# A hybrid attention and mixture-of-experts step: the samples' attention taken batch by batch, with one ring of five key/value buffers and two expert units loaded behind slots 3 and 8

## The chip, the cores and the metric

The kernel runs on one core of a Trainium2 chip. The metric is the device time of one execution in microseconds; the median of three runs of the kernel before is 1143.01 us. TensorE, VectorE, ScalarE and GpSimd compute; SyncE here only issues DMAs, and waits for semaphores before it does.

## The reference, cut to what matters

One layer of a decoder in float32 for 256 prompt tokens and 32 sample tokens (8 batches of 4), with D = 1024.

```python
proj = x_all @ w_in                       # q, k, v of two head groups (A and B), 8 heads of 64 each
oa_p, ob_p = attention(prompt)            # 256 x 256, causal, ALiBi; group B weights dilated patterns
oa_s = attention(q_s, [cache_k[pages], k_s], [cache_v[pages], v_s])       # per batch: 256 past keys + 4 new
ob_s = attention(q_s, [state_k_win, k_s], [state_v_win, v_s])
hx = layer_norm(ALPHA * x_all + head_rmsnorm([oa, ob]) @ w_out)
comb = top4(softmax(hx @ w_router + b_router))
f = sum(comb[:, e] * (swiglu(hx @ w_gate_up[e] + b_gate_up[e]) @ w_down[e] + b_down[e]) for e in range(32))
y = layer_norm(ALPHA * hx + f)
```

The 32 experts' weights are 403 MB and are read once. The 16 key and 16 value blocks of the samples (8 batches, two groups) are 256 x 512 floats each, 512 KB.

## The kernel before, in words

**Attention in slots.** The first stage is written out by hand in 29 slots (`STEPS`, L276). Every engine walks the same slots in order, each with its own part of each. In slots 0 to 23 TensorE makes one eighth-width piece of the projection (`project`, L747, products at L764 and L767, and at L773 for the samples' values in slots 11 and 23); in slots 24 to 28 it multiplies with `w_out` (L925, samples L930). Behind that product, tables (L277 to L284) say what else a slot has: `SCORE`, `TURN`, `MIX`, `MSQ` for the prompt's eight head pairs, `KROWS` for turning key rows that are to be stored (`turn_rows`, L814), and `KEY`, `SAMP_SCORE`, `SAMP_TURN`, `SAMP_MIX` for the samples.

**The samples' attention** comes in four quads: group A or B, and batches 0 to 3 or 4 to 7. A key block `m` (0 to 15) is turned by eight transposes (`turn_keys`, L827, transposes at L737): four of its first 128 positions into PSUM bank 5, four of its other 128 into bank 6. ScalarE copies bank 5 and VectorE bank 6 into `kT[m % 6]` (`copy_keys`, L1469 and L1739). When four blocks are turned, `samp_scores` (L838) makes the quad's scores in one go, 16 matmuls of 256 columns and 16 of 32, each on one of four 32-column tiles of the array, one tile per batch. VectorE adds and takes the maximum, ScalarE exponentiates, VectorE scales (`samp_scale`), TensorE turns the probabilities (`samp_turn`, L860) and ScalarE copies them to `sampPT` (L1489). `samp_mix` (L866) multiplies with the values, 12 matmuls of 512 columns for all eight heads of a batch at once, and VectorE keeps the right head of each row (`samp_take`, L1760): a masked copy over 512 columns and a sum.

**Buffers.** SyncE loads key blocks into a ring of four (`kring`) and values a quad at a time, 2 MB (`vring`, loads 0, 1, 2 to one place and load 3 to the key ring's). These lie over the expert ring: nine slots of 16 KB per partition (`ring`), of which slot 0 holds the values in this stage, slot 1 four of the six `kT`, slots 2 to 4 `xT`, `qkT` and `vtok`, slot 5 the key ring, slots 6 and 7 the weights `wblk` and `wout`.

**The hand-over to the experts.** A unit is 2 MB of expert weights; a pair of experts has 12 units (8 of `w_gate_up`, 4 of `w_down`), and there are 16 pairs. After attention's own loads SyncE issues the first pair's units as their places come free, each behind a wait, in this order: unit 1 when all sample scores are made, 0 when three quads are mixed, half of unit 6 (to a place aside, `first`), 5 when the last quad is mixed, 2 when the last mean squares are made, 3 and 4 when everything that leaves `qkT`, `vtok` and `kstage` has been stored (L557), 9 behind the first residual sums, 7 and 8 when `w_out`'s products are done, the other half of 6, and then 10, 11 and those of the next pair, each when the unit that held its slot has been used (`unit_free`, L569). The product of pair 0 with `w_gate_up` (L1176) begins at 219 us in the profiled execution. From there on all is loops over pairs: gather (L1060), gate and up (L1176), down (L1229), combine (L1256).

**Order around slots 18 to 28.** In slot 19 VectorE takes the reciprocal of the first four pairs' mean squares (`invert_means`, L1788) and scales the first samples' rows (`samp_norm`, L1805). Its key copy stands early in a slot, before the sample sums. In slot 27 two reciprocals over 512 columns (`scale_out`, L1781) follow the last head pair's mixing of slot 26.

Of the kernel before, what the change touches and what calls it, by code (L numbers as in the profile page):

```python
# [16 lines left out]
SEQ = 256  # L17
# [20 lines left out]
KRING, KTURNED = 4, 6  # L38
# [25 lines left out]
def constant_tables():  # L64
# [7 lines left out]
    keep[p, C_HEAD + p // DS % H] = 1  # L72
# [11 lines left out]
    b, h, q = p // NS, p // DS % H, p % DS  # L84
# [25 lines left out]
def build_layer(nc, x_prompt, x_sample, cache_k, cache_v, state_k, state_v, page_table, w_in, gn_moba,  # L110
# [9 lines left out]
    def place(name, shape, at=None, dt=F32):  # L120
# [16 lines left out]
    sampM = place("sampM", [128, G], at=acc_at + 10240)  # L137
# [49 lines left out]
    vring = [place("vring0", [128, 4, 2, G], at=at[0])] * 3 + [place("vring3", [128, 4, 2, G], at=at[5])]  # L187
    kT = [place(f"kT{m}", [128, 4, PAST], at=(at[6] + 24576 if m < 2 else at[1] - 8192) + 4096 * m) for m in range(KTURNED)]
    xT = place("xT", [128, KC, T], at=at[2])
    headPT.append(place("headPT2", [128, 2, 384], at=at[2] + 9216))  # L190
    sampPT = place("sampPT", [128, 2, 3, 128], at=at[2] + 12288)
    square = place("square", [128, SEQ], at=at[2] + 15360)
# [3 lines left out]
    kring = place("kring", [128, KRING, 2, G], at=at[5])  # L196
# [4 lines left out]
    qblk = place("qblk", [128, 2, DB, 4, 32])  # L201
# [4 lines left out]
    sampP = place("sampP", [128, SW])  # L206

# [3 lines left out]
        wout_in2 wout_in3 k_landed0 k_landed1 k_landed2 k_landed3 v_landed0 v_landed1 v_landed2 v_landed3 ln1_in  # L211
# [22 lines left out]
    k_landed = [sems[f"k_landed{i}"] for i in range(KRING)]  # L234
    v_landed = [sems[f"v_landed{i}"] for i in range(4)]
# [40 lines left out]
    SLOTS_P, STEPS = 2 * len(BLOCKS), 29  # L276
    SCORE = {4: 0, 6: 1, 8: 2, 10: 3, 16: 4, 18: 5, 20: 6, 22: 7}  # L277
# [124 lines left out]
    def _(sp):  # L402
# [36 lines left out]
        def load_k(m):  # L439
            if m >= KRING:  # L440
                sp.wait_ge(S.keys_turned, 2 * (m - KRING + 1))
            load_keys(m, (pages_k, win_k), kring[:, m % KRING], k_landed[m % KRING])

        def load_v(q):
            if q in (1, 2):
                sp.wait_ge(S.samp_mixed, q)
            if q == 3:
                sp.wait_ge(S.keys_turned, 32)
            for b4 in range(4):
                load_keys(4 * q + b4, (pages_v, win_v), vring[q][:, b4], v_landed[q])  # L450
# [6 lines left out]
        load_k(0)  # L457
        load_w_in(2)
        for m in range(1, KRING):
            load_k(m)  # L460
        load_v(0)
# [3 lines left out]
        def free_slot(m):  # L465
            return [s for s, n in KEY.items() if n == m - KRING][0]

        for slot in range(1, SLOTS_P):
            for n in range(3, len(BLOCKS)):
                if 2 * (n - 3) + (3 if BLOCKS[n - 3][1:] == (2, 0) else 1) == slot:  # L470
                    load_w_in(n)
            if slot == 19:
                sp.wait_ge(S.projected, 20)
                load_wout(0)
            for m in range(KRING, 16):
                if free_slot(m) == slot:
                    load_k(m)
            if slot in (14, 18):
                load_v(SAMP_MIX[slot] + 1)

# [15 lines left out]
        def load_start(u):  # L496
            load_unit(0, 0, u, slot=start_slot(u))

# [34 lines left out]
        load_v(3)  # L533
# [12 lines left out]
        sp.wait_ge(S.samp_mixed, 4)  # L546
# [110 lines left out]
    def _(pool):  # L657
# [9 lines left out]
        def block_queries(g):  # L667

            pool.wait_ge(S.proj_copied, copied_at(slot_of_tile(g, 0, 3)))
            for j in range(4):  # L670
                for half in range(2):
                    r = slice(64 * half, 64 * half + 64)
                    nc.gpsimd.tensor_copy(
                        qblk[r, g, :, j, 8 * j + 4 * half:8 * j + 4 * half + 4],
                        qkT[r, 8 * g + j, SEQ:T].rearrange("p (b q) -> p b q", b=DB)).then_inc(S.qblk_ready, 1)
# [23 lines left out]
        nc.gpsimd.memset(qblk[:], 0.0).then_inc(S.qblk_ready, 1)  # L699
        pool.wait_ge(S.projected, 4)  # L700
        copy_state(2)
        pool.wait_ge(S.qblk_ready, 1)
# [32 lines left out]
    def _(pe):  # L735
# [78 lines left out]
        def turn_rows(i, slot):  # L814
# [3 lines left out]
            pe.wait_ge(S.keys_copied_act, jobs_to(KEY, slot))  # L818
            if i:
                pe.wait_ge(S.kstage_ready, i)  # L820
            if i == 3:
                pe.wait_ge(S.samp_taken, 3)
# [4 lines left out]
        def turn_keys(m, slot):  # L827
            pe.wait_ge(k_landed[m % KRING], 32 * (m // KRING + 1))
            for c in range(2):
                if m:  # L830
                    pe.wait_ge((S.keys_copied_act, S.keys_copied_dve)[c], m)
                if c == 0 and jobs_to(KROWS, slot):
                    pe.wait_ge(S.kstage_ready, jobs_to(KROWS, slot))
                for j in range(4):
                    ins = turn(bank[5 + c][:, 128 * j:128 * j + 128], kring[:, m % KRING, c, 128 * j:128 * j + 128])
                ins.then_inc(S.keys_turned, 1)

        def samp_scores(q):  # L838

            g, quad = divmod(q, 2)  # L840
            if q == 1:
                pe.wait_ge(S.samp_copied, 2)
            if q == 2:
                pe.wait_ge(S.samp_taken, 2)
            if q == 3:
                pe.wait_ge(S.samp_copied, 6)
            pe.wait_ge(S.qblk_ready, 8 * g + 9)
            pe.wait_ge(S.proj_copied, copied_at(slot_of_tile(g, 1, 3)))
            pe.wait_ge(S.keys_copied_act, 4 * q + 4)
            pe.wait_ge(S.keys_copied_dve, 4 * q + 4)  # L850
            for part in range(2):
                for j in range(4):
                    for b4 in range(4):
                        out = bank[7][32 * b4:32 * b4 + 32, 0:PAST] if part == 0 else bank[7][32 * b4:32 * b4 + 32, PAST:SW]
                        k = kT[(4 * q + b4) % KTURNED][:, j, :] if part == 0 else qkT[:, 8 * g + 4 + j, SEQ:T]
                        ins = nc.tensor.matmul(out, qblk[:, g, 4 * quad + b4, j, :], k, start=(j == 0), stop=(j == 3),
                                               tile_position=(0, 32 * b4))
            ins.then_inc(S.samp_scored, 1)
# [7 lines left out]
        def samp_mix(q):  # L866
            g = q // 2
            pe.wait_ge(S.samp_copied, (4, 4, 6, 8)[q])
            pe.wait_ge(S.vtok_ready, 8 * g + 8)
            pe.wait_ge(v_landed[q], 128)  # L870
            if q == 1:
                pe.wait_ge(S.samp_taken, 1)
            if q == 2:
                pe.wait_ge(S.kstage_ready, 3)
                pe.wait_ge(S.keys_copied_act, 16)
# [17 lines left out]
        def head_mix(n):  # L893
# [6 lines left out]
            elif n:  # L900
                pe.wait_ge(S.keys_copied_dve, 16)
# [1356 lines left out]
```

## Time and profile before

| | us |
|---|---|
| median of three runs | 1143.01 |
| the three runs | 1143.07, 1141.0, 1143.01 |
| span of the profiled execution | 1138.4 |
| TensorE busy | 1100.8 |
| VectorE busy | 293.2 |
| ScalarE busy | 204.1 |
| first product with expert weights starts at | 219.0 |

The profile shows one execution; its span runs from the first to the last instruction, and the runs' times hold some 4.6 us more, at its start and end. Matmuls are pipelined, and a busy TensorE is not TensorE at its peak. TensorE's granted clock is full for nearly the whole span (mean 0.997).

### The profile page before, as it was taken

The page shows a single profiled execution, that of the slowest core. Times are in us where ns is not written, and L with a number is a line of the kernel's source. Part 1 is how long each engine was busy: PE and PEld are TensorE (multiplying, and loading weights), DVE is VectorE, ACT ScalarE, POOL GpSimd, SP SyncE. Part 2 cuts the span into 40 slices and gives each one's busy share as a digit, 9 for nine tenths or more (in the row PEclk, how much of TensorE's full clock was granted, in tenths as well). Part 3 has the DMA queues.
Part 4 walks back from the last instruction along what each step waited for, and adds up shares of the span by engine and source line. Part 5 has one row for each costly group of instructions (what it writes and reads, how often), then busy time and mean ns, then how long its engine had stood idle before and what let it go on. Part 6 is the DMA issues. An engine that isn't in the chain of part 4 may idle for free.

```text
span 1138.4 us, 14132 instructions
## 1 busy us (share of the span) xinstructions
PE 1100.8 (97%) x5468; PEld 462.9 (41%) x5469; DVE 293.2 (26%) x734; ACT 204.1 (18%) x481; POOL 30.2 (3%) x65
## 2 busy tenths in 40 slices
PE   8999999999999999999999999999999999999996
PEld 6876764433333333333333333333333333333331
DVE  1553757530303030212121212121202031303123
ACT  2322412411111120202020202020201111111112
POOL 0110111000000000000000000000000000000001
PEclk9999999999999999999999999999999999999998
DMA  9967778999999999999999999999999999999994
GB/s 361 347 221 247 286 274 344 418 431 408 429 420 425 432 431 430 430 430 431 432 429 431 432 431 432 431 431 431 431 431 432 432 431 431 431 430 430 397 423 192
DMA packets 61348, 454.37 MB, mean 399 GB/s; under 512 B 6595, under 2 KB 19539, under 8 KB 35572
## 3 DMA queue, kind: packets, MB, share of 16 engines
q1 hardware_dynamic: 58818, 440.97, 93.0%
q0 software_dynamic: 1728, 10.75, 2.5%
q10 hardware_dynamic: 754, 1.98, 0.4%
q8 instruction: 34, 0.56, 0.2%
q14 instruction: 14, 0.11, 0.0%
HBM read 450.14 MB, written 11.93 MB: 406 GB/s over the span
## 4 chain that ended last, share of the span: by engine, by line
PE 79%; DMA 16%; ACT 2%; DVE 1%; SPq 1%; issue 1%; DVEq 0%
PE bank L1176 26%; PE bank L1229 19%; DMA ring<-in_w_gate_up 15%; PE bank L737 6%; PE bank L764 6%; PE bank L1060 5%; PE bank L1256 3%; PE bank L1344 2%; PE bank L767 2%; PE bank L925 2%; PE bank L1056 1%; DMA ln_bs<-in_ln_b 1%; PE bank L882 1%; PE bank L1272 1%; ACT ybuf L1448 1%; ACT actT L1448 1%
## 5 line engine op out<-in xcount | busy, mean ns | idle before, releaser
L1176 PE MATMUL bank<-ring,xg 128*64 128x512 f32 x1904 | 417.6, 594 | 11.2 <-DMA ring<-in_w_gate_up 11.2
L1176 PEld LDWEIGHTS bank<-ring,xg 128*64 128x64 f32 x1904 | 137.6, 137 | 282.0 <-issue 279.8
L1229 PE MATMUL bank<-ring,actT 128*64 128x512 f32 x960 | 216.1, 597 | 4.1 <-ACT actT L1448 4.1
L2111 DVE TENSOR_TENSOR acc<-acc,bank 128x512 f32<-128x512 f32 x60 | 41.3, 688 | 484.8 <-PE bank L1256 484.7
L1602 ACT ACTIVATE sig<-gate 128x256 f32<-128x256 f32 x64 | 26.7, 417 | 526.0 <-DVE gate L2093 526.0
L1229 PEld LDWEIGHTS bank<-ring,actT 128*64 128x64 f32 x960 | 67.3, 137 | 119.9 <-issue 115.3
L2093 DVE TENSOR_SCALAR gate<-bank 128x256 f32<-128x256 f32 x64 | 26.9, 420 | 194.8 <-PE bank L1176 175.8
L764 PE MATMUL bank<-xT,wblk 128*128 128x288 f32 x256 | 65.4, 409 | 0.2 <-DVE xT L1701 0.2
L1593 ACT ACTIVATE xg<-bank,small 128x128 f32<-128x128 f32 x128 | 48.1, 457 | 97.0 <-PE bank L737 96.9
L1060 PE MATMUL bank<-hx,pick 128*128 128x512 f32 x128 | 59.2, 605 | 0.0
L1448 ACT ACTIVATE ybuf<-bank 128x512 f32<-128x512 f32 x63 | 36.0, 596 | 126.8 <-PE bank L1229 87.3
L1256 PE MATMUL bank<-ybuf,spread 128*128 128x512 f32 x120 | 58.4, 618 | 0.0
L764 PEld LDWEIGHTS bank<-xT,wblk 128*128 128x128 f32 x256 | 47.4, 190 | 14.6 <-issue 2.7
L1060 PEld LDWEIGHTS bank<-hx,pick 128*128 128x128 f32 x128 | 23.0, 189 | 34.3 <-issue 34.3
L1256 PEld LDWEIGHTS bank<-ybuf,spread 128*128 128x128 f32 x120 | 19.1, 188 | 39.0 <-DVE acc L2111 19.7
L925 PE MATMUL bank<-wout,outT 128*128 128x512 f32 x64 | 29.8, 603 | 0.0
L767 PE MATMUL bank<-wblk,xT 128*128 128x256 f32 x128 | 29.1, 380 | 0.0
L1344 PE MATMUL bank<-ring,xg 128*64 128x512 f32 x128 | 28.3, 595 | 0.0
L2097 DVE SCALAR_TENSOR_TENSOR up<-up,gate 128x256 f32<-128x256 f32 x64 | 27.2, 425 | 3.3
L737 PEld LDWEIGHTS bank<-keep,ybuf 128*128 128x128 f32 x128 | 17.7, 207 | 25.3 <-issue 24.3
L728 POOL TENSOR_TENSOR acc<-acc,ln_b_sb 128x512 f32<-128x512 f32 x2 | 3.0, 1502 | 941.5 <-DVE acc L2217 941.5
L2094 DVE TENSOR_SCALAR up<-bank 128x256 f32<-128x256 f32 x64 | 26.6, 415 | 0.0
(249 smaller groups left out, 707.5 us busy)
## 6 DMA issues: line engine op xcount, KB each, us to landing
ring<-in_w_gate_up SPq DMA_DIRECT2D x119, 2048.0 KB, 26.5
ring<-in_w_down SPq DMA_DIRECT2D x63, 2048.0 KB, 27.3
ring<-in_w_gate_up SPq DMA_DIRECT2D x16, 1024.0 KB, 20.1
wblk<-in_w_in SPq DMA_DIRECT2D x11, 1024.0 KB, 7.8
kring<-in_cache_k_moba SPq DMA_DIRECT2D x16, 256.0 KB, 7.3
vring<-in_cache_v_moba SPq DMA_DIRECT2D x16, 256.0 KB, 7.3
out<-in_state_k_win POOLq DMA_DIRECT2D x8, 512.0 KB, 5.0
out<-in_state_v_win POOLq DMA_DIRECT2D x8, 512.0 KB, 5.9
```

Source lines behind the costliest of these rows:

```text
L737: return nc.tensor.transpose(out, in_, ident[0:in_.shape[0], 0:in_.shape[0]])
L764: ins = nc.tensor.matmul(out[:, 0:T], w[:, k, 128 * c:128 * c + 128], xT[:, k, :], start=(k == 0), stop=(k == KC - 1))
L767: ins = nc.tensor.matmul(out[:, 0:256], xT[:, k, 128 * c:128 * c + 128], w[:, k, :], start=(k == 0), stop=(k == KC - 1))
L925: return nc.tensor.matmul(bank[2 * t + half][:, :], outT[:, k, t0:t0 + rows], wout[:, k, 512 * half:512 * half + 512], start=(k == 0), sto ...
L1060: return nc.tensor.matmul(bank[6 + a][:, :], pick[:, t, :], hx[:, t, 512 * a:512 * a + 512], start=False, stop=(t == 1))
L1176: ins = nc.tensor.matmul(bank[n][64 * e:64 * e + 64, :], xg[:, k, 64 * e:64 * e + 64], w[e][:, 512 * n:512 * n + 512], start=False, stop=( ...
L1229: ins = nc.tensor.matmul(bank[4 + half][64 * e:64 * e + 64, :], actT[:, j, 64 * e:64 * e + 64], w[e][:, at:at + 512], start=(j == 0), stop ...
L1256: ins = nc.tensor.matmul(bank[4 + half][:, :], spread[:, t0:t0 + rows], ybuf[:, 512 * half:512 * half + 512], start=True, stop=True)
L1344: ins = nc.tensor.matmul(bank[n][64 * e:64 * e + 64, :], xg[:, k, 64 * e:64 * e + 64], w[:, at:at + 512], start=False, stop=(k == KC - 1))
L1448: return nc.scalar.activation(out, in_, ACT.Copy, **kw)
L1593: ins = nc.scalar.activation(xg[:, k, :], turned, ACT.Identity, bias=s_(c_cols + KC + k), scale=s_(c_cols + k))
L2111: V.tensor_tensor(o, o, new, ALU.add).then_inc(S.added, 1)
```

## The change

Scores and mixing go batch by batch. The four tiles of the array now hold the four head pairs of one batch, where they held the four batches of a quad. So a key block can be scored as soon as it is turned (`KSCORE`), two `kT` buffers do, and a value block can be used when it lands. Keys and values share one ring of five 512 KB buffers, `kv`; four of them lie where the key ring lay, one in the ninth slot. A buffer is loaded when the use five places earlier in the list `KV_USED` is over. The products with the values are 36 matmuls of 128 columns a quad, in two parts (`MIX_FIRST`, `MIX_LAST`). Both halves of a key block go through bank 5: the first behind the slot's projection, the second at the slot's end, after ScalarE has copied the first. VectorE's key copy moves to the end of the slot. Slots 0 and 1 of the expert ring are free in this stage, and SyncE issues unit 0 in its slot 3 and unit 1 in its slot 8.

```diff
-KRING, KTURNED = 4, 6
+KVRING, KTURNED = 5, 2
...
+    EARLY_UNITS = {3: 0, 8: 1}
-    KEY = {1: 0, 2: 1, 3: 2, 4: 3, 5: 4, 6: 5, 10: 6, 11: 7, 13: 8, 15: 9, 16: 10, 17: 11, 19: 12, 20: 13, 21: 14, 22: 15}
-    KROWS = {8: 0, 12: 1, 14: 2, 25: 3, 26: 4, 27: 5}
-    SAMP_SCORE, SAMP_TURN = {9: 0, 12: 1, 20: 2, 23: 3}, {10: 0, 13: 1, 21: 2, 24: 3}
-    SAMP_MIX = {14: 0, 18: 1, 24: 2, 26: 3}
+    KEY = {4: 0, 5: 1, 7: 2, 8: 3, 9: 4, 10: 5, 12: 6, 14: 7, 15: 8, 16: 9, 18: 10, 19: 11, 20: 12, 21: 13, 22: 14, 23: 15}
+    KSCORE = {7: (0,), 8: (1,), 9: (2,), 10: (3,), 12: (4,), 13: (5,), 14: (6,), 15: (7,), 18: (8,), 19: (9,), 20: (10, 11),
+              22: (12,), 23: (13,), 24: (14, 15)}
+    KROWS = {11: 0, 13: 1, 17: 2, 24: 3, 25: 4, 26: 5}
+    SAMP_SUM, SAMP_TURN = {10: 0, 15: 1, 20: 2, 24: 3}, {11: 0, 16: 1, 21: 2, 25: 3}
+    MIX_FIRST, MIX_LAST = {12: 0, 17: 1, 22: 2, 26: 3}, {13: 0, 18: 1, 23: 2, 26: 3}
+    MIX_AT = ((6, 0), (6, 0), (6, 0), (7, 384))
...
# SyncE
+        def load_kv(n):
+            v, m, _ = KV_USED[n]
+            if n >= KVRING:
+                v_before, before, _ = KV_USED[n - KVRING]
+                if v_before:
+                    sp.wait_ge(S.samp_mixed, before // 2 + 1)
+                else:
+                    sp.wait_ge(S.keys_turned, 2 * before + 2)
+            load_keys(m, ((pages_k, win_k), (pages_v, win_v))[v], kv[n % KVRING], kv_landed[n % KVRING])
...
-        load_v(3)
         sp.wait_ge(S.projected, SLOTS_P)
         load_wout(1)
         load_wout(2)
-        sp.wait_ge(S.samp_scored, 4)
+        sp.wait_ge(S.samp_scored, 16)
         load_wout(3)
-        load_start(1)
-        sp.wait_ge(S.samp_mixed, 3)
-        load_start(0)
...
# TensorE
+        def turn_keys(m, c, slot):
+            if c == 0:
+                pe.wait_ge(*kv_in(0, m))
                 if m:
+                    pe.wait_ge(S.keys_copied_dve, m)
+                if jobs_to(KROWS, slot):
                     pe.wait_ge(S.kstage_ready, jobs_to(KROWS, slot))
+            else:
+                pe.wait_ge(S.keys_copied_act, m + 1)
+            for j in range(4):
+                ins = turn(bank[5][:, 128 * j:128 * j + 128], kv_of(0, m)[:, c, 128 * j:128 * j + 128])
+            ins.then_inc(S.keys_turned, 1)
...
+            for j in range(4):
+                ins = nc.tensor.matmul(bank[7][32 * j:32 * j + 32, 0:PAST], qblk[:, quad, window(b4, j)], kT[m % KTURNED][:, j, :],
+                                       start=(b4 == 0), stop=False, tile_position=(0, 32 * j))
...
+            for b4 in (2 * part, 2 * part + 1):
+                pe.wait_ge(*kv_in(1, 4 * q + b4))
+                for c in range(2):
+                    for j in range(4):
+                        ins = nc.tensor.matmul(out[32 * j:32 * j + 32, :], sampPT[:, c, window(b4, j)],
+                                               kv_of(1, 4 * q + b4)[:, c, 128 * j:128 * j + 128],
+                                               start=(b4 == 0 and c == 0), stop=False, tile_position=(0, 32 * j))
...
# TensorE's order within a slot: project, turn_keys(m, 0), scores, mean squares, head scores, turn_rows,
# samp_turn, mixing parts, head_turn, head_mix, spread_means, turn_samples, turn_keys(m, 1)
+            if slot in KEY:
+                turn_keys(KEY[slot], 1, slot)
...
# ScalarE and VectorE, before the copy of key block m
-                act.wait_ge(S.samp_scored, (m - KTURNED) // 4 + 1)
+                act.wait_ge(S.samp_scored, m - KTURNED + 1)
...
# VectorE, in samp_take
-            link(V.tensor_reduce(otS[:, q, :], sampM[:, :].rearrange("p (h d) -> p d h", h=H), AXX, ALU.add))
+            link(V.tensor_tensor(otS[:, q, :], sampM[:, 0:64], sampM[:, 64:128], ALU.add))
...
# VectorE, last in its slot
+            if slot in KEY:
+                copy_keys(KEY[slot])
```

The lines that begin with # say where a piece stands. The tables that hold batch and head numbers, and GpSimd's copies of the queries into `qblk` (four larger ones for eight), follow the new order of rows.

## Rows read from the trace of the kernel before

**Rows 1.** The page: TensorE's busy time, and GB/s in 40 equal slices.
```profile
PE 1100.8 (97%) x5468; PEld 462.9 (41%) x5469; DVE 293.2 (26%) x734; ACT 204.1 (18%) x481; POOL 30.2 (3%) x65
...
GB/s 361 347 221 247 286 274 344 418 431 408 429 420 425 432 431 430 430 430 431 432 429 431 432 431 432 431 431 431 431 431 432 432 431 431 431 430 430 397 423 192
```
**Rows 2.** TensorE's longest wait up to 215 us and from 660 us: us, times, longest.
```profile
PE bank L737 <- DMA keep<-in_keep_table: 4.9, 1, 4.9
...
PE bank L1176 <- DMA ring<-in_w_gate_up: 11.2, 11, 1.3
```
**Rows 3.** Windows: length, engines' busy us, then TensorE's clock, DMA share, GB/s.
```profile
194.00:196.00 2.00, 2.00 (x5) 0.57 (x3) 1.86 (x7) 0.00 (x0) 0.00 (x0) 1.00 0.00 0
...
660.00:1095.00 435.00, 419.49 (x1868) 150.52 (x1864) 79.45 (x186) 60.08 (x137) 0.00 (x0) 1.00 1.01 428
```
**Rows 4.** SyncE's timeline at the hand-over (start us, us), and one of its waits.
```profile
158.41 7.40 SPq L494 DMA_DIRECT2D ring<-in_w_gate_up  x2
...
183.86 12.42 SPq L494 DMA_DIRECT2D ring<-in_w_gate_up  x3
...
222.61 0.37 SPq L494 DMA_DIRECT2D ring<-in_w_down  x1
...
SPq L557 <- DMA out<-kstage: 11.0, 1, 11.0
```
**Rows 5.** Tile `ring`, time from issue to landing: unit 3 (195.4 us), unit 10 (222.6 us).
```profile
DMA to landing us min/median/max: 7.2/7.2/7.2
...
DMA to landing us min/median/max: 8.0/8.0/8.0
```
**Rows 6.** The chain in order of time in the attention stage: start us, us, what.
```profile
80.13 2.16 PE bank L856 x62
...
93.54 2.84 PE bank L882 x24
...
108.64 3.88 PE bank L764 x16
...
114.85 4.08 PE bank L764 x16
...
153.29 1.88 PE bank L773 x64
```
**Rows 7.** Tiles `kT` (ScalarE) and `sampM` (VectorE): duration ns min/median/max.
```profile
L1448 ACT ACTIVATE kT<-bank x16: 597/598/600, 18.6 to 148.4; 128x512 f32<-128x512 f32 x16
...
L1762 DVE TENSOR_TENSOR sampM<-bank,keep x4: 681/692/692, 96.5 to 179.0; 128x512 f32<-128x512 f32 x4
```
**Rows 8.** Timelines of TensorE and VectorE in slots 19 to 21: start us, us.
```profile
127.09 1.04 PE L737 MATMUL bank<-keep,kring 128*128 128x128 f32 x8
...
130.75 1.75 DVE L1790 RECIPROCAL msq<-msq 128x256 f32<-128x256 f32 x1 [0.64 <-ACT msq L1504]
...
132.77 0.42 DVE L1708 COPY vtok<-bank 128x256 f32<-128x256 f32 x1
...
133.68 0.56 DVE L1722 SCALAR_TENSOR_TENSOR headS<-bank,headB 128x384 f32<-128x384 f32 x1
...
136.51 0.68 DVE L1743 COPY kT<-bank 128x512 f32<-128x512 f32 x1
...
139.87 0.16 DVE L1748 RECIPROCAL small<-small 128x1 f32<-128x1 f32 x1
...
141.50 0.49 PE L737 MATMUL bank<-keep,sampP 128*128 128x128 f32 x3
```
**Rows 9.** Timelines from the last head pair's mixing on: start us, us.
```profile
178.89 0.65 PE L910 MATMUL bank<-headPT,vtok 128*64 128x256 f32 x4
...
182.72 3.35 DVE L1784 RECIPROCAL msq<-msq 128x512 f32<-128x512 f32 x1
...
191.62 0.69 DVE L1785 TENSOR_TENSOR outT<-outT,msq 128x512 f32<-128x512 f32 x1
...
192.40 3.70 PE L925 MATMUL bank<-wout,outT 128*128 128x512 f32 x8
```

More of the change, by code:

```diff
@@ L195, in build_layer @@
     kstage[0] = place("kstage0", [128, G], at=at[3] + 30720)
-    kring = place("kring", [128, KRING, 2, G], at=at[5])
+    kv = [place(f"kv{n}", [128, 2, G], at=at[5] + 4096 * n if n < 4 else top_at + 4096) for n in range(KVRING)]
     wblk = place("wblk", [128, 3, KC, 256], at=at[6])
@@ L280, in build_layer, with kv_in, kv_of, window @@
     MSQ = {12: 0, 14: 1, 16: 2, 18: 3, 23: 4, 25: 5, 26: 6, 27: 7}
-    KEY = {1: 0, 2: 1, 3: 2, 4: 3, 5: 4, 6: 5, 10: 6, 11: 7, 13: 8, 15: 9, 16: 10, 17: 11, 19: 12, 20: 13, 21: 14, 22: 15}
-    KROWS = {8: 0, 12: 1, 14: 2, 25: 3, 26: 4, 27: 5}
-    SAMP_SCORE, SAMP_TURN = {9: 0, 12: 1, 20: 2, 23: 3}, {10: 0, 13: 1, 21: 2, 24: 3}
-    SAMP_MIX = {14: 0, 18: 1, 24: 2, 26: 3}
+    KEY = {4: 0, 5: 1, 7: 2, 8: 3, 9: 4, 10: 5, 12: 6, 14: 7, 15: 8, 16: 9, 18: 10, 19: 11, 20: 12, 21: 13, 22: 14, 23: 15}
[5 more added lines that the diff above has]
+    MIX_AT = ((6, 0), (6, 0), (6, 0), (7, 384))
+    KV_USED = []
+    for slot in range(STEPS):
+        if slot in KEY:
+            KV_USED.append((0, KEY[slot], slot))
+        for part, table in enumerate((MIX_FIRST, MIX_LAST)):
+            if slot in table:
+                KV_USED += [(1, 4 * table[slot] + 2 * part + n, slot) for n in range(2)]
+    KV_AT = {(v, m): n for n, (v, m, _) in enumerate(KV_USED)}
+    def kv_in(v, m):
+        n = KV_AT[v, m]
+        return kv_landed[n % KVRING], 32 * (n // KVRING + 1)
+    def kv_of(v, m):
+        return kv[KV_AT[v, m] % KVRING]
+    def window(b4, j):
+        return slice(120 * b4 + 32 * j, 120 * b4 + 32 * j + 32)
     def is_v(slot):
@@ L497, in load_start @@
             load_unit(0, 0, u, slot=start_slot(u))
+        for slot in range(1, SLOTS_P):
+            for n in range(3, len(BLOCKS)):
+                if 2 * (n - 3) + (3 if BLOCKS[n - 3][1:] == (2, 0) else 1) == slot:
+                    load_w_in(n)
+            if slot == 19:
+                sp.wait_ge(S.projected, 20)
+                load_wout(0)
+            for n in range(KVRING, len(KV_USED)):
+                if KV_USED[n - KVRING][2] == slot:
+                    load_kv(n)
+            if slot in EARLY_UNITS:
+                load_start(EARLY_UNITS[slot])
         def load_whole(p, odd, u):
@@ L669, in block_queries @@
             pool.wait_ge(S.proj_copied, copied_at(slot_of_tile(g, 0, 3)))
-            for j in range(4):
+            if g:
+                pool.wait_ge(S.samp_scored, 8)
+            for quad in range(2):
                 for half in range(2):
@@ L833, in turn_keys @@
                     pe.wait_ge(S.kstage_ready, jobs_to(KROWS, slot))
[L834 to L857, printed above, removed]
@@ new lines, in turn_keys, with samp_scores @@
+            else:
[3 more added lines that the diff above has]
+            ins.then_inc(S.keys_turned, 1)
+        def samp_scores(m):
+            g, quad, b4 = key_jobs[m]
+            if b4 == 0:
+                pe.wait_ge(S.qblk_ready, 4 * g + 6)
+                if m:
+                    pe.wait_ge(S.samp_copied, 3 * (m // 4))
+            pe.wait_ge(S.keys_copied_act, m + 1)
+            pe.wait_ge(S.keys_copied_dve, m + 1)
+            for j in range(4):
+                ins = nc.tensor.matmul(bank[7][32 * j:32 * j + 32, 0:PAST], qblk[:, quad, window(b4, j)], kT[m % KTURNED][:, j, :],
+                                       start=(b4 == 0), stop=False, tile_position=(0, 32 * j))
+            if b4 == 3:
+                pe.wait_ge(S.proj_copied, copied_at(slot_of_tile(g, 1, 3)))
+                for n in range(4):
+                    for j in range(4):
+                        ins = nc.tensor.matmul(bank[7][32 * j:32 * j + 32, PAST:SW], qblk[:, quad, window(n, j)],
+                                               qkT[:, 8 * g + 4 + j, SEQ:T], start=False, stop=(n == 3),
+                                               tile_position=(0, 32 * j))
@@ L975, in _ @@
                 ins.then_inc(S.gn_turned, 1)
+            if slot in KEY:
+                turn_keys(KEY[slot], 0, slot)
+            for m in KSCORE.get(slot, ()):
+                samp_scores(m)
             if slot in MSQ:
```

164 lines of the change are left out of this document (68 added, 96 removed).

## The prediction

> **What bounds the kernel now.** I read the page first, then TensorE's waits by stretch, the DMA share by stretch, SyncE's issues around the hand-over from attention to the experts, and last the slots of the attention stage engine by engine. The page: TensorE is busy all through, DMA moves some 430 GB/s from the eighth slice on but only 221 to 286 in slices three to six [rows 1]. TensorE's waits split the run in two. Up to 215 us its only long one is 4.9 us for the first table; after 660 us it waits 11.2 us in eleven pieces for `ring<-in_w_gate_up` [rows 2]. So attention, up to the first expert product at 219 us (call that moment G), is TensorE's own work, and the last 435 us follow the weight stream at 428 GB/s [rows 3].
>
> The question is therefore whether the stream, from which 4 MB are taken, really runs further ahead. A unit is 2 MB, 4.87 us at the 431 GB/s of most slices [rows 1]. Before, units 1 and 0 are issued at 158.4 and about 165 us, units 3 and 4 at the end of the piece that began at 183.86 (at 195.4 and 195.8), because SyncE stood 11.0 us for the stores of `kstage` [rows 4]. At 194 to 196 us the DMA engines move nothing [rows 3]: what was queued before that moment is done, and taking 9.7 us of loads out of it moves nothing behind it. Unit 10 is issued at 222.61 us [rows 4], when the product on unit 0's slot has ended (G + 3.6): at G the ring is full, before as after. Its landing took 8.0 us; a unit issued on an idle queue took 7.2 [rows 5]. **That 0.8 us is all that the stream can gain against G**; its later end follows unit 10.
>
> **The change part by part.** First, TensorE's instructions.
> - Mixing: a quad's product with the values took 2.84 us, 12 matmuls of 512 columns. It becomes 36 of 128. The nearest row is the projection of the samples, 32 matmuls of 128 columns on 32-column tiles in 1.88 us: 36 make 2.1, and with a switch between the two parts 2.15. Four quads: -2.8 us [rows 6].
> - Scores: the same 32 matmuls a quad (2.16 us), but in 14 places instead of 4. Each place begins and ends with a change between the full array and 32-column tiles. Such a change costs 0.1 us: a projection between full-array neighbours takes 3.88 us, between tiled ones 4.08 [rows 6]. Ten more places, about 0.12 each: +1.2 us. (bounds: 0 and 10 x 0.2 = 2.0)
> - Key transposes: 16 batches of eight become 32 of four. Each batch gets one more change (16 x 0.1), but the second half now stands last in its slot, so that the next projection follows full-array work: some 16 times 3.88 in place of 3.98 or 4.08. Together +0.2 us.
> - The third set of key rows moves from slot 27 into 26, ahead of the last head's mixing: 4 transposes, +0.4 us.
> Sum: -1.0 us.
> The Trainium skill, page TensorEngine Tiling (Array Packing), section Key Properties, says that changing the tiling mode drains the array, which speaks against ten more places. If each drain cost the whole 0.2 us by which the two projections differ, the sum would be +0.8 us higher; the rows show half of that a change.
>
> Second, **the copies of the keys, now through one bank and two buffers.** TensorE waits in each batch until ScalarE has taken the first half out of bank 5 before it turns the second. The copy takes 0.60 us [rows 7], the end of the transposes and the semaphores about 0.3, so 0.9 us must be covered by what stands between the halves: a burst of scores 0.45, a head's transposes 0.7, head scores 0.86, a mixing part 1.0. From the tables: slots 8, 10, 12, 14 to 16, 18, 20 to 23 have over 0.9 us there; slots 4 and 5 fall short by 0.1 and 0.25; in slots 7, 9 and 19 the copy itself waits for the scores two batches back, which frees `kT`, and falls short by 0.15 each. +0.8 us, taken as 0.7. Bounds: 0 and, with no cover in any batch, 16 x 0.9 = 14 us.
>
> Third, **VectorE's half of the copy moves to the end of its slot.** The next first half waits for it. Mostly a projection (3.5 to 3.9 us) covers it. Not in slot 19: there VectorE takes the reciprocal of the mean squares, 1.75 us from 130.75, and the sample norms until 132.8 us, then goes on with slot 20's values [rows 8]. The copy of 0.69 us now stands behind these, so it ends at 133.8, while TensorE, which ends slot 19's projection at 127.1 and has 5.7 us of work until slot 20's projection is done, wants it at 132.8: wait 1.0 us. Slot 20 then scores two batches before the head scores. From the head scores VectorE has 1.5 us until it may start its first pass, 2.8 for the front (133.68 to the copy at 136.51), 0.9 for the sample sums, 0.6 for a scaling, 0.7 for the key copy, then 1.3 and 0.55 for the two scalings (before, the sample one began at 139.87) [rows 8]: 7.9 us from the start of the head scores to the sample transposes of slot 21. TensorE has 6.4 between them (0.86, 0.97, 0.5, 3.5, 0.5). Wait 1.45 us. Before, the same transposes stood at 141.50, over 1 us behind their input, and nothing waited. Together +2.4 us. Bounds: 0 (other slack) and 4 (VectorE's 5 copies of slot 21 to 23 late as well).
> VectorE's cheaper sample take (its pass of 0.69 us over 512 columns becomes one over 128 [rows 7]) is on no path.
>
> At the last head's mixing (178.89 us before [rows 9]) this gives -1.0 + 0.7 + 2.4 = +2.1 us. From there to the end of attention the chain is not TensorE's: VectorE takes two reciprocals of 3.35 us, the first from 182.72, and the product behind the second runs from 191.62 to 192.3; TensorE goes on at 192.40 [rows 9]. The key rows, now a slot earlier, save TensorE some 1 us there, VectorE nothing; I count -0.2. **G: +1.9 us.**
>
> Fourth, SyncE and the queues. Keys and values share five buffers; the shortest notice is the eleventh value batch, issued when the fourteenth key batch has been turned at the end of slot 22 and used in slot 23 behind 5.4 us of projection, 1 us of keys and scores and 0.6 of mean squares; 2 MB landed in 7.2 us on an idle queue [rows 5], of which 4.87 are its bytes, so two loads of 256 KB need some 3.5: hidden on the nearly idle queue of that stretch; cost 0, up to 2 with a unit's worth ahead of them. Units 0 and 1 are issued behind slots 3 and 8. Slots 1 to 3 lose their key work, and of the first loads 1.5 MB less is queued; a weight block has four slots (16 us or more) until use, so 4.9 us of a unit ahead of it is hidden: cost 0, up to 2 us without that cover. GpSimd's four larger copies replace eight of 0.2 us and have a projection as cover: 0. Units 3 and 4 start 5 us earlier (the stores end earlier), and stand ready earlier than they are used.
>
> **The sum.** +1.9 (G) - 0.8 (stream against G) = +1.1 us. The profiled execution has a span of 1138.4 us, 4.6 below the median of 1143.01; I take the outside as unchanged. Forecast 1144.1 us. About 0.2% (2.3 us) is what a measurement here can tell from no change, so the likeliest answer is "no difference", with a lean to slower.
>
> **Rivals.**
> *The stream leads after all* (faster). If the 4 MB taken out did carry through, up to 9.7 us less stream would meet 11.2 us of waits: with G at +1.9 the end comes at 9.7 - 1.9 = 7.8 less, 1135 us. For it: the 11.2 us are there to be had. Against: the empty stretch at 194 to 196 us and unit 10's gate. 0.06.
> *The hand-over of bank 5 is paid in full* (slower). Place: the second half's wait for ScalarE in `turn_keys`. Price: 0.9 us a batch less cover. It decides once ScalarE reaches the copy over 0.5 us late (exponentials of the slot before, which end shortly before the next projection), for half the batches: 8 x 0.9 = +7 us, 1151. Against: before, each half waited in the same way for the copy of the batch before, and TensorE never stood for it [rows 2]. 0.18.
> *VectorE has more slack than I read*: no 2.4 us in slots 20 and 21, and G falls to -0.5, the time to 1141.7; still not told from no change, but near it. 0.16. Its low end (no switching cost either) is 1140.3.
> *The change does nothing to the stream because the early units hold up weight blocks*: priced above at 2 us; in the range.
> My own case 0.60, its range 1141.5 to 1147.5.
>
> **Chances.** Faster by over 0.2%: 0.06 from the stream, 0.05 from VectorE's slack, 0.05 from my case: 0.16. Slower: 0.18 from bank 5, 0.12 from my case: 0.30. The rest 0.54. The range takes in my case, the slack case and the lower part of the bank 5 case: 1140.0 to 1149.0.
>
> **What would show it.** Right: DMA engines with nothing to move in some stretch between 170 and 210 us, unit 10 issued at G + 3.6 and landing in some 7.2 us, G 1 to 3 us later, TensorE's waits up to 215 us of 2 to 4 us in all, by `kT` copies of VectorE in slot 20 and by `sampP` in slot 21, and waits for weights after 660 us of about 10. Wrong: a wait on ScalarE's copies in most of 16 batches; G earlier than 219; waits for weights gone to 1 or 2 us.

## The result, and the profile after

The changed kernel takes 1155.48 us (median; its runs lie from 1154.51 to 1156.24), the kernel before 1142.87 in the same comparison: a ratio of 1.0122, 95% interval 1.0110 to 1.0134. It is 12.6 us slower, and outside the range. The profiled execution has a span of 1152.4 us, 14.0 more than before, and 11.66 of these are there when the first expert product starts (G: 230.58 us for 218.92). (Every execution on record, of both kernels and of all runs below, takes 1.8 to 2.3 us more than its span. The 4.6 us of the section on the time before compare one execution's span with the median of others.)

The page after, TensorE's busy time and the queue that brings instructions, answers to [rows 1]:
```profile
PE 1107.7 (96%) x5660; PEld 468.2 (41%) x5661; DVE 288.0 (25%) x734; ACT 204.1 (18%) x485; POOL 28.3 (2%) x58
...
q8 instruction: 53, 0.87, 0.3%
```
The same queue on the page of the kernel before:
```profile
q8 instruction: 34, 0.56, 0.2%
```
TensorE's waits after, up to 215 us (us in total, times, longest), answer to [rows 2]:
```profile
PE bank L949 <- DMA wout<-in_w_out: 4.8, 1, 4.8
...
PE bank L758 <- DVE sampP L1781: 1.1, 1, 1.1
PE bank L758 <- issue: 1.0, 2, 0.8
PE bank L949 <- DVE outT L1818: 0.8, 1, 0.8
PE bank L758 <- ACT kT L1476: 0.2, 1, 0.2
```
And from 660 us on:
```profile
PE bank L1088 <- issue: 2.6, 1, 2.6
...
PE bank L1084 <- issue: 2.0, 1, 2.0
PE bank L1204 <- DMA ring<-in_w_gate_up: 1.5, 2, 1.0
```
Three things stand out. There is a new wait of 4.8 us for a piece of `w_out`, the longest of the attention stage. The waits for weights fell from 11.2 us to 1.5, and yet the kernel is slower. And in their place stand waits for "issue": TensorE waits for nothing that the profile shows. The early units are not to blame for the first: SyncE's timeline after (start us, us) answers to [rows 4].
```profile
147.65 19.20 SPq L462 DMA_DIRECT2D kv<-in_state_v_win  x12
166.89 1.82 SPq L550 DMA_DIRECT2D bias_rows<-in_b_gate_up  x4
168.75 1.46 SPq L476 DMA_DIRECT2D wout<-in_w_out  x3
...
190.74 0.37 SPq L499 DMA_DIRECT2D ring<-in_w_gate_up  x1
```
Twelve loads of values go out one by one as buffers of the ring of five come free, the last at 166.4 us, behind slot 23's mixing (done at 163.8 us) and its last key transposes (165.1). The second quarter of `w_out` stands behind them and the four loads of biases in program order, and is issued at 168.75 us, though its place is free once slot 23's projection is done. The chain of waits and the windows show what that did:
```profile
168.75 7.49 DMA wout<-in_w_out
176.29 5.66 PE bank L949 x8
```
```profile
174.00:176.00 2.00, 0.00 (x0) 0.00 (x0) 0.00 (x0) 0.00 (x0) 0.00 (x0) 0.50 0.96 330
176.00:178.00 2.00, 1.71 (x2) 0.84 (x3) 0.00 (x0) 0.00 (x0) 0.00 (x0) 0.50 1.02 416
```
TensorE stands idle from 171.5 to 176.3 us, its granted clock falls to 0.50 (1.2 GHz) while it does, and the eight products that follow start at that level and take 5.66 us, where the eight of the slot before took 3.60.

The other stop is at the loop over three pairs. TensorE's timeline around its first jump back:
```profile
594.61 1.13 PE L1084 MATMUL bank<-hx,pick 32*128 32x512 f32 x4 [1.81 <-issue]
595.66 1.12 PE L1088 MATMUL bank<-hx,pick 128*128 128x512 f32 x2
600.10 2.93 PE L1088 MATMUL bank<-hx,pick 128*128 128x512 f32 x3 [3.31 <-issue]
```
```profile
600.00:604.00 4.00, 3.90 (x5) 1.70 (x6) 0.00 (x0) 0.60 (x1) 0.00 (x0) 0.57 1.02 438
```
Two gaps of 1.81 and 3.31 us, then a clock of 0.57 over four microseconds; the same happens at the second jump back, near 765 us, with gaps of 1.95 and 2.62 us. From one pair's first expert product to the next it is 55.7 us in this stretch, and 62.8 and 62.6 us across the two jumps. In the kernel before there is no such gap.

### The profile page after: what moved, and what is told of

It reads as the page before. It is cut to its first block, busy times and chain, and to the rows that moved or that the text cites. A ratio compares the mean times of both kernels' runs of the same rounds, so it can differ in the third digit from the quotient of the medians.

```text
span 1152.4 us, 14531 instructions
## 1 busy us (share of the span) xinstructions
PE 1107.7 (96%) x5660; PEld 468.2 (41%) x5661; DVE 288.0 (25%) x734; ACT 204.1 (18%) x485; POOL 28.3 (2%) x58
## 4 chain that ended last, share of the span: by engine, by line
PE 90%; DMA 3%; DVE 2%; ACT 2%; issue 2%; SPq 0%; ACTq 0%; DVEq 0%
PE bank L1204 34%; PE bank L1257 19%; PE bank L758 6%; PE bank L785 6%; PE bank L1088 5%; PE bank L1284 5%; PE bank L1372 2%; DMA ring<-in_w_gate_up 2%; PE bank L788 2%; PE bank L949 2%; PE bank L1084 1%; PE bank L1300 1%; PE bank L1405 1%; ACT ybuf L1476 1%; ACT actT L1476 1%
## 5 line engine op out<-in xcount | busy, mean ns | idle before, releaser
L1204 PEld LDWEIGHTS bank<-ring,xg 128*64 128x64 f32 x1904 | 135.2, 137 | 272.9 <-issue 272.8
L1088 PE MATMUL bank<-hx,pick 128*128 128x512 f32 x128 | 63.4, 638 | 5.9 <-issue 5.9
```

What stands on the lines that cost most here:

```text
L1088: return nc.tensor.matmul(bank[6 + a][:, :], pick[:, t, :], hx[:, t, 512 * a:512 * a + 512], start=False, stop=(t == 1))
L1204: ins = nc.tensor.matmul(bank[n][64 * e:64 * e + 64, :], xg[:, k, 64 * e:64 * e + 64], w[e][:, 512 * n:512 * n + 512], start=False, stop=( ...
```

## The experiments

All runs are of whole kernels; none leaves out part of the computation.

**SyncE's order** (`wout_ahead`).
```diff
+            if slot == 23:
+                sp.wait_ge(S.projected, SLOTS_P)
+                load_wout(1)
             for n in range(KVRING, len(KV_USED)):
...
         sp.wait_ge(S.projected, SLOTS_P)
-        load_wout(1)
         load_wout(2)
```


> SyncE's order alone: the second quarter of w_out is issued as soon as slot 23's projection is done, ahead of the two value loads that wait for slot 23's keys and mixing. Theory 1 (SyncE's queue): in the changed kernel TensorE stood 4.8 us for that quarter, and the eight products behind it took 5.66 us at a partly halved clock where three windows of full clock give about 3.5. Both go: first expert product 6.9 us earlier, near 223.8 us in the trace, and the time falls from 1155.5 to about 1148.5 us. Rival (TensorE would be held by the samples' mixing or by the last reciprocals anyway): the first expert product comes less than 2 us earlier and the time stays above 1153.5.

Measured: 1147.68 us, 7.8 less; against before 1.0057 (1.0044 to 1.0069). The wait is gone from TensorE's waits, and its timeline runs on:
```profile
163.26 3.60 PE L951 MATMUL bank<-wout,outT 128*128 128x512 f32 x8
...
169.72 3.60 PE L951 MATMUL bank<-wout,outT 128*128 128x512 f32 x8
...
175.25 3.70 PE L951 MATMUL bank<-wout,outT 128*128 128x512 f32 x8
```
From the first of these to the third it is 12.0 us; after the change it was 19.0 (164.90 to 183.87). So 7.0 us belong to this one place in SyncE's queue (the edit puts the load ahead of the biases too). Theory 1 holds, the rival falls. The first expert product came at 223.66 us, as expected, though two other differences of this execution lie in that number and cancel: its first slots ran 1.6 us faster, and its first gather 1.7 us slower (the last section).

**VectorE's order** (`vector_order`).
```diff
+            if slot == 21:
+                samp_scale(SAMP_TURN[slot])
             if slot in TURN:
                 head_scale(TURN[slot])
-            if slot in SAMP_TURN:
+            if slot in SAMP_TURN and slot != 21:
                 samp_scale(SAMP_TURN[slot])
...
             if slot == 19:
+                copy_keys(KEY[slot])
                 samp_squares(0)
...
-            if slot in KEY:
+            if slot in KEY and slot != 19:
                 copy_keys(KEY[slot])
```


> VectorE's order alone: in slot 19 the key copy goes ahead of the reciprocals, in slot 21 the scaling of the samples' probabilities ahead of that of the head's. Theory 2 (VectorE's late copies): the stops of 0.95 us in slot 20 and about 1.5 us in slot 21 go; the first expert product comes 2.4 us earlier, the time is about 1153.1 us. Rival (the wait only moves to the next thing that VectorE owes TensorE, since its work is only reordered): less than 1 us.

Measured: 1153.19 us, 2.3 less; 1.0103 (1.0087 to 1.0118) against before. First TensorE's timeline after the change, then that of this run:
```profile
131.05 3.62 PE L788 MATMUL bank<-wblk,xT 128*128 128x256 f32 x16
135.45 0.63 PE L758 MATMUL bank<-keep,kv 128*128 128x128 f32 x4 [0.78 <-issue]
...
145.11 0.55 PE L758 MATMUL bank<-keep,sampP 128*128 128x128 f32 x3 [1.12 <-DVE sampP L1781]
145.50 0.82 PE L758 MATMUL bank<-keep,headS 128*128 128x128 f32 x6
```
```profile
131.26 3.62 PE L788 MATMUL bank<-wblk,xT 128*128 128x256 f32 x16
134.71 0.60 PE L758 MATMUL bank<-keep,kv 128*128 128x128 f32 x4
...
143.07 0.52 PE L758 MATMUL bank<-keep,sampP 128*128 128x128 f32 x3
143.70 1.21 PE L758 MATMUL bank<-keep,headS 128*128 128x128 f32 x6
```
From slot 20's projection to slot 21's sample transposes it is 11.8 us for 14.1: both stops were VectorE's order of work. Some 0.6 us of the 2.3 come back at once, since the head's scaling now stands behind the samples': the head's six transposes begin later and wait in their middle, 1.21 us for 0.82. Slot 22's projection starts 1.6 us sooner, measured from slot 20's. Theory 2 holds for the two stops, and the rival for a quarter of what they gave. The time resolves this only roughly: the six runs lie between 1150.62 and 1155.69 us, and the interval overlaps that of the changed kernel. The first expert product, expected 2.4 us sooner, came at 231.46 us, 0.9 later than after the change. In this execution the clock stayed low longer behind the stop for `w_out` (8.6 us for 7.6 from that slot's product to the next slot's), and fell once more ahead of the first gather (1.7 us, the last section).

**The loop's place in the instruction stream.** The first pair of runs put no-operations ahead of the loop.
```diff
                     if k == KC - 1:
                         ins.then_inc(S.gate_up_done, 1)
+                    for _ in range(2):
+                        if isinstance(i, int) and 0 < i < 4 and room[0] > 0:
+                            pe.nop()
+                            room[0] -= 1
```


> 64 no-operations are put between expert products of TensorE's stream ahead of the loop over three pairs, nothing else. Theory 3 (place of the loop in the instruction stream): in the changed kernel the loop's jump back is followed twice by a stop of some 7 us, with blocks of 16 KB on the instruction queue all through the loop; in the kernel before that queue is silent from 570 to 940 us. By counting TensorE's records against those blocks the loop begins late in a block after the change and early in one before. 64 more instructions move it into the next block: both stops go, the queue is silent for two rounds of the loop, the waits for weights after 660 us come back (1.5 us to about 11) and the time falls by what was not covered, 2 to 2.5 us, to about 1153.2. Rival (the stops belong to the changed order of buffers or to a weight unit): they stay, and the time is 1155.5 to 1157.

> The kernel before with 152 no-operations in the same place, which puts its loop late in a block of the instruction stream. Theory 3: two stops of 6 to 7 us at the jumps back, near 585 and 765 us, instruction blocks through the whole loop, waits for weights after 660 us down from 11.2 us to 1 or 2, and the time 1.5 to 3 us above that of the kernel before, about 1145. Rival (the stops come from what the change moved, not from where the loop lies): no stop, 1143. A second rival (the no-operations themselves cost TensorE time): the pairs before the loop take longer than 55.8 us each.

Measured: 1155.25 and 1141.48 us (1.0121 and 0.9999 against before), stops as in the kernels they were made from. The number of instructions on their pages is unchanged (14531 and 14132): the no-operations never reached the chip. They settle nothing of the theory, and serve as a repeat of both kernels. With a wait on a semaphore that has long come in their place (`pe.wait_ge(S.ident_in, 16)`; five in one place make two instructions, and the eleven of the run with 392 make five) the stream really grows.

> The earlier pair with no-operations was no test: TensorE executed exactly as many instructions as without them (11763 records, instruction blocks at the same records), so they never reached the stream. Here waits on a semaphore that has long come stand in their place, 64 more instructions ahead of the loop over three pairs. Theory 3 (place of the loop in the instruction stream): both stops of 6 to 7 us at the jumps back go, the instruction queue is silent for two rounds of the loop, waits for weights after 660 us rise from 1.5 to about 11 us, the time falls by 2 to 2.5 us to about 1153. Rival (the stops belong to what the change moved in the buffers): they stay, time 1155.5.

> The kernel before with 152 more such instructions in TensorE's stream ahead of the loop, which puts the loop's end where it lies after the change, late in a block of 16 KB. Theory 3: two stops of 6 to 7 us behind the loop's jumps back, instruction blocks all through the loop, waits for weights after 660 us down from 12 us to 1 or 2, and the time 1 to 3 us above that of the kernel before, 1143 to 1145 where that is 1142. Rival: no stop and 1142. Second rival (the waits cost TensorE time): the pairs before the loop take longer than 55.8 us.

Measured: after with 64 more, 1152.1 us (1.0093, 1.0080 to 1.0106), 3.2 to 3.4 less than without. Its instruction queue, its waits from 660 us on, and the jump:
```profile
q8 instruction: 36, 0.59, 0.2%
```
```profile
PE bank L1206 <- DMA ring<-in_w_gate_up: 11.9, 12, 1.3
```
```profile
582.75 8.32 PE L1206 MATMUL bank<-ring,xg 128*64 128x512 f32 x38
591.00 1.13 PE L1084 MATMUL bank<-hx,pick 32*128 32x512 f32 x4
```
The stops are gone, no instruction block is fetched between 581 and 957 us, and the waits for weights are back at their old size: the stops had only hidden them. Not all of the 3.2 to 3.4 us is the stops', though: from the first expert product to the end of the span the seven profiled executions with stops (of all runs here) take 921.8 to 923.2 us, and the six without 919.5 to 921.1, some 2.3 us less. The changed kernel's profile also has 1.8 us of slow first slots, which that with 64 waits has not (the last section). The kernel before with 152 more gave 1141.27 us (0.9997), no stop, 34 blocks as ever. Theory 3 held in one kernel and missed in the other, so either its zone was drawn too wide or place alone was not the cause. Three more runs were made to tell: two kernels before with 392 and 136 more, one after with 32 more.

> The kernel before with 392 more instructions (waits that have long come) ahead of TensorE's loop: the loop then begins at the same instruction of the stream, number 5320, as in the changed kernel. With 152 more it showed no stop, so 'late in a block' alone was not it. Theory 3a (the place in the stream, whatever the kernel does): two stops of 6 to 7 us behind the jumps back, waits for weights after 660 us fall from 12 us to 1 or 2, and the time is 2 to 3 us above the kernel before, near 1144.5. Rival (the place alone does nothing; the stop needs something else of the changed kernel, and the 64 instructions removed it by timing): no stop, 1142.

> The kernel before with 136 more instructions ahead of the loop: its place within a block of 256 instructions is that of the changed kernel, one block-number apart. Theory 3b (only the place within a block counts, in a zone less than 16 instructions wide, since 152 more lay outside it): two stops as in the changed kernel, time near 1144.5. Theory 3c (the number of the block counts too): no stop, 1142.

> The changed kernel with 32 more instructions ahead of the loop in place of 64; the loop's last instruction becomes the first of a block. By the narrow zone that 152 more in the kernel before left (its loop ended 16 instructions further into a block than the changed kernel's): no stops, time near 1152.5 as with 64. Rival (a wide zone that depends on the block number): the stops stay, 1155.5.

Measured: before with 392, 1144.05 us (1.0022, 1.0012 to 1.0032); before with 136, 1144.57 us (1.0022, 1.0013 to 1.0031); after with 32, 1152.2 us (1.0094). The kernel before, with none of the change and 136 idle waits, has the stops of the changed one:
```profile
582.61 1.13 PE L1056 MATMUL bank<-hx,pick 32*128 32x512 f32 x4 [1.81 <-issue]
...
588.38 2.08 PE L1060 MATMUL bank<-hx,pick 128*128 128x512 f32 x2 [3.59 <-issue]
```
```profile
PE bank L1060 <- issue: 2.3, 1, 2.3
...
PE bank L1178 <- DMA ring<-in_w_gate_up: 1.2, 2, 0.9
```
By these two runs of the kernel before, with 392 and 136 more, the stops cost 2.0 and 2.5 us.

The loop is 1561 instructions long, 64 bytes each in the compiled programs; blocks are 16 KB (0.56 MB in 34), so 256 instructions. Where its last instruction lies, counted in the compiled programs:

| kernel | last instruction | place in its block | stops, blocks fetched |
|---|---|---|---|
| before | 6488 | 88 | none, 34 |
| before + 136 | 6624 | 224 | two, 52 |
| before + 152 | 6640 | 240 | none, 34 |
| after; before + 392 | 6880 | 224 | two, 53 |
| after + 32 | 6912 | 0 | none, 36 |
| after + 64 | 6944 | 32 | none, 36 |

Theory 3b holds as far as these seven programs go: three of them end their loop at place 224 and stop, one with the change and two without it, and none of the four others does. The zone ends between 224 and 240. Where it begins, between 88 and 224, was not tried, and why it lies there is not shown. The change brings TensorE 392 more instructions (192 products with their weight loads and 8 waits), and moved the loop from 88 to 224 by chance.

The Trainium skill, page Runtime: NRT & Kernel Launch, section Instruction fetch mechanics, says that instructions come in blocks of 16 KiB and that a taken branch whose target isn't in the engine's window forces a fetch before execution goes on. These runs agree in part: blocks of 16 KB follow each jump that stops. The same section puts that window at two pages, and there the runs differ: the loop lies in seven blocks (in eight with 32 more), and at four of the five places tried its jumps back fetch none of them. That the outcome turns on 16 instructions of place the page does not say.

**The early units** (`units_late`).
```diff
-            if slot in EARLY_UNITS:
-                load_start(EARLY_UNITS[slot])
...
         load_wout(3)
+        load_start(1)
+        load_start(0)
```


> The changed kernel without the early units: units 1 and 0 are issued behind the last quarter of w_out, near 168 us, and not behind slots 3 and 8; all else stays. My prediction's claim (the 4 MB taken out move nothing): first expert product and time within 1 us of the changed kernel, 1155.5. Rival 1 (the early units do help the stream): slower by 2 us or more. Rival 2 (they hold up weight blocks or keys and values in the attention stage): faster by 1 us or more. The later units may stand longer behind these 4 MB, since unit 5 is issued only near 190 us; I expect it covered.

Measured: 1156.18 us (1.0125, 1.0110 to 1.0139), 0.7 more than the changed kernel, inside both intervals. The second rival falls: the early units hold up nothing. The first falls by its own measure, 2 us of the time, but the trace speaks for a help in another place than the stream. Here the units' 4 MB are issued right behind `w_out`'s second quarter, which lands 9.4 us after its issue for 7.5, and TensorE waits 6.7 us for it, for 4.8. The first expert product comes at 231.79 us, where `after_64_waits` and `after_32_waits`, alike up to there but for the early units, have 228.86 and 227.35. The changed kernel's own 230.58 hides this by its slow first slots. So the early units relieve the load that SyncE issues late; how much of it reaches the time is open.

**All three corrections** (`all_three`): the two edits of order, and the 64 waits.

> The changed kernel with all three corrections: w_out's second quarter ahead, VectorE's order, the loop moved by 64 instructions. If the three costs are separate they add up: w_out 7 us, VectorE 2.3 us, the stops at the loop 2 to 2.5 us: first expert product near 221.5 us in the trace (219.5 where TensorE's clock is full from the start), time 1155.5 - 11.5 = 1144. What is left against the kernel before, some 2 us, would be the scores' and transposes' extra changes and the wait before slot 20's samples. Rival (a further limit behind them): more than 1147.

Measured: 1142.29 us; against before 1.0011 (1.0001 to 1.0020). The medians add up: 7.8 + 2.3 + 3.4 = 13.5 us singly, 13.2 together (12.7 by the ratios to the kernel before, whose median is 1141.78 in this comparison). The spans say what these hold: this one is 12.5 us shorter than the changed kernel's, 7.0 for `w_out`, 1.6 for VectorE, 2.1 behind the first expert product, and 1.8 for the slow first slots, which no edit touched. TensorE's waits up to 215 us and from 660 us on:
```profile
PE bank L760 <- DMA keep<-in_keep_table: 4.7, 1, 4.7
PE bank L951 <- DVE outT L1826: 0.8, 1, 0.8
```
```profile
PE bank L1208 <- DMA ring<-in_w_gate_up: 11.0, 10, 1.3
```
This is the change without the two costs that my prediction missed, and without VectorE's stops, which it had; it costs 0.1%. It does not beat the kernel before.

## Why the prediction was wrong

**The step that failed** is the fourth, "SyncE and the queues ... cost 0, up to 2". I looked at how much notice each new load gets, and found the shortest one hidden. I did not ask what stands behind the waits that guard those loads. Before, the late values were one batch of loads; now SyncE walks a list of buffers, each with a wait of its own, up to slot 23's mixing and keys, and `w_out`'s second quarter, which needs only slot 23's projection, is behind it. It cost 4.8 us of wait, 2.1 us of halved clock, and 7.8 us of the time. My "what is queued behind the waiting instruction" was answered for VectorE and TensorE, and for SyncE only for the loads themselves.

**A cost that no step named** is the loop's place in the stream: two stops of about 7 us. That they cost 2.0 to 3.4 us and not 14 is the stream's doing: 11.2 us of waits for weights [rows 2] were there to be used up, and fell to 1.5.

**The sum in the profiled executions.** G came 11.66 us later: 7.0 for `w_out`, 1.6 for VectorE's order (net), 1.8 for the slow first slots, and 1.25 that stay in `all_three` (220.17 us for 218.92). Behind G the span is 2.3 us longer, for the stops at the jumps. The slow first slots are this execution's clock, no step of mine; whether the median holds them is not shown.

**VectorE's copies, +2.4 us**: right in place, and about right in size. In slot 20 TensorE stood 0.78 us (forecast 1.0; the profile gives it to "issue", and it went with the copy's order), in slot 21 1.12 (forecast 1.45). Undone: 2.3 us at the place and in the median, 1.6 net in the trace.

**Bank 5, +0.7 us, and its rival of +7**: 0.2 us in all, the last row of the waits. ScalarE's copies were covered nearly everywhere.

**TensorE's instructions, -1.0 us**: wrong by some 1.7 us. `all_three` has VectorE's stops removed, and its last head mixing starts at 180.19 us for 178.89 [rows 9], its first product 0.2 us sooner: +1.5 us, where -1.0 + 0.7 = -0.3 was forecast. Of the 1.5 us 0.6 are the head transposes that the new order makes wait, and 0.2 bank 5, which leaves +0.7 for the instructions. Groups by form of the kernel before, 9.3 to 196 us:
```profile
L737 PE MATMUL bank<-keep,kring 128*128 128x128 f32 x128 | 17.1, 276 | 0.0
L856 PE MATMUL bank<-kT,qblk 128*32 128x256 f32 x128 | 7.7, 382 | 0.0
L882 PE MATMUL bank<-vring,sampPT 128*32 128x512 f32 x64 | 7.7, 598 | 0.0
...
L882 PE MATMUL bank<-vtok,sampPT 32*32 32x512 f32 x32 | 4.2, 600 | 0.0
```
and of `all_three`:
```profile
L760 PE MATMUL bank<-keep,kv 128*128 128x128 f32 x128 | 20.0, 278 | 0.4 <-ACT kT L1484 0.2 <-issue 0.2
L871 PE MATMUL bank<-kT,qblk 128*32 128x256 f32 x128 | 9.8, 390 | 0.0
L901 PE MATMUL bank<-kv,sampPT 128*32 128x128 f32 x256 | 8.8, 275 | 0.0
...
L907 PE MATMUL bank<-vtok,sampPN 32*32 32x128 f32 x32 | 1.7, 280 | 0.0
```
Neighbouring groups overlap in these sums, so they overstate, but they say where it is: the keys' transposes +2.9 (forecast +0.2: cutting each batch in two costs more than the change of tiles), the scores +2.1 (forecast +1.2), the mixing -1.4 (forecast -2.8; the last quad took 2.23 us from its first product to the next work for 2.84, but the other three stand in two places each).

**The tail, -0.2 us**: nearly right; +1.30 us at the last mixing is +1.25 at the first expert product of `all_three`.

**The stream, -0.8 us**: its marks were all there. The DMA engines were idle before the hand-over, and unit 10 was issued 3.6 us behind the first expert product and landed in 7.3 us:
```profile
186.00:188.00 2.00, 2.00 (x8) 1.00 (x7) 0.91 (x2) 0.00 (x0) 0.00 (x0) 1.00 0.00 0
```
```profile
234.28 3.80 SPq L499 DMA_DIRECT2D ring<-in_w_down  x2
```
But from the first expert product to the end of the span `all_three` needs 919.7 us (1139.9 - 220.17) and the kernel before 919.5 (1138.4 - 218.92): the 0.8 us did not reach the end. Where it went I did not follow.

The mark that I had set for being wrong, "waits for weights gone to 1 or 2 us", was met, but not by the stream that it was meant for.

## What to carry to other kernels

When a ring of large buffers becomes a ring of small ones, its loads turn into a list of waits; walk down the issuing queue and ask of each other load behind them when it could have gone. A change that adds instructions ahead of a long loop can move that loop onto a place where each jump back fetches it anew: look at the instruction queue's count on the page and for "issue" gaps behind the jump, and shift the loop before judging the change. And where the end follows a stream, a stop costs only what exceeds the waits it swallows, here 2.0 to 3.4 of 14 us.

## What the runs showed of the hardware

- **The jump back.** Behind a jump that is followed by fetches TensorE stands 1.8 to 2.4 us, works 2.2 to 3.1 us, stands another 2.3 to 3.6 us, and then runs at a granted clock near 0.5 for some microseconds (both jumps of the seven profiled executions with stops). Sixteen instructions of place make the difference (`before_136_waits`, `before_152_waits`).
- **The clock after idle time.** It fell to 0.50 (1.2 GHz) within the 4.8 us in which TensorE stood. It also fell in two executions with no wait of TensorE right before, behind a stretch of small products just ahead of the first gather. In `vector_order` and `wout_ahead` the gather's eight products took 5.38 us, in the changed kernel itself, with the same stretch ahead, 3.68 (windows of `wout_ahead`, then the gathers of `vector_order` and of the changed kernel):
```profile
217.00:219.00 2.00, 2.00 (x4) 0.88 (x4) 1.60 (x10) 0.00 (x0) 0.00 (x0) 0.53 1.00 414
```
```profile
224.72 5.38 PE L1088 MATMUL bank<-hx,pick 128*128 128x512 f32 x8
```
```profile
225.54 3.68 PE L1088 MATMUL bank<-hx,pick 128*128 128x512 f32 x8
```
- **The first slots.** TensorE's first 32 projections took 9.8 to 9.9 us in three of the thirteen profiled executions (the changed kernel, `after_64_nops`, `vector_order`) and 8.00 in the ten others, `wout_ahead` among them, which does the same as the changed kernel up to there. The trace shows no wait in it, but products at half the pace up to 13.0 us. The products between 9 and 13 us, duration in ns (min/median/max), in the changed kernel and in `wout_ahead`:
```profile
L785 PE MATMUL bank<-xT,wblk x8: 481/684/817, 9.4 to 12.9; 128*128 128x288 f32 x8
```
```profile
L787 PE MATMUL bank<-xT,wblk x14: 406/406/481, 9.5 to 12.8; 128*128 128x288 f32 x14
```
The first record of a full clock stands at 13.0 to 13.2 us in those three executions and at 7.8 to 9.4 in the ten others: an execution can start 1.8 us slower because its clock rises later, and why it does is not shown. Two profiles of different kernels are to be compared from a common point behind it.
